# A streaming encoder layer on one core: two heads' prompt states computed behind the output projection, and the gated output turned one step later

## What is computed

```python
s_new = s * jnp.exp(L * log_gamma)[None, :, None, None] + jnp.einsum(
    'blhd,blhv->bhdv', k * k_decay[None, :, :, None], v)
```

## Time and profile before

| | us |
|---|---|
| median of 3 runs | 1492.9 |
| lowest and highest | 1490.93, 1495.36 |
| the profiled execution, its own time | 1492.03 |
| its span, first to last instruction | 1489.8 |
| TensorE busy | 1461.5 |
| VectorE busy | 837.7 |
| ScalarE busy | 659.5 |
| POOL busy | 303.2 |

### The profile page before, as it was taken

How to read it: one execution, slowest core, us unless ns; L and a number is a source line. 1 busy time by engine, 2 the same in 40 slices (tenths; PEclk the granted TensorE clock), 3 DMA queues, 4 the chain that set the end, 5 groups by cost and what they waited for, 6 DMA issues and landing times.

```text
span 1489.8 us, 21889 instructions
## 1 busy us (share of the span) xinstructions
PE 1461.5 (98%) x8004; PEld 1158.5 (78%) x8004; DVE 837.7 (56%) x1456; ACT 659.5 (44%) x1083; POOL 303.2 (20%) x181
## 2 busy tenths in 40 slices
PE   8999999999999999999999999999999999999998
PEld 6777787778777877787877677777888888887885
DVE  3532532253225222221866778655365899988998
ACT  5323312331233123322446545645233478888883
POOL 1352233224313431233000000000321100001004
PEclk9999999999999999999999999999999999999999
DMA  9646565555556455433441353245831799999996
GB/s 324 216 125 204 170 192 140 187 191 184 158 185 208 144 167 197 161 99 91 159 142 43 111 168 133 71 153 178 276 124 43 267 372 404 403 365 402 399 393 230
DMA packets 156460, 304.61 MB, mean 204 GB/s; under 512 B 16752, under 2 KB 54520, under 8 KB 155972
## 3 DMA queue, kind: packets, MB, share of 16 engines
q1 hardware_dynamic: 152548, 292.72, 58.2%
q0 software_dynamic: 3808, 10.49, 2.0%
HBM read 258.45 MB, written 47.86 MB: 206 GB/s over the span
## 4 chain that ended last, share of the span: by engine, by line
PE 45%; DMA 4%; DVE 2%; issue 1%; ACT 1%; POOL 0%; DVEq 0%; ACTq 0%; SPq 0%; POOLq 0%
PE pj L93 11%; PE pj L95 11%; PE pj L94 11%; DMA m_raw<-w 2%; PE d_B L2731 1%; PE d_B L2758 1%; PE d_B L2750 1%; DMA d_kc<-cache_diff_k 1%; PE d_B L2792 1%; PE d_B L2740 1%; PE d_B L2898 1%; PE d_B L2719 1%; PE d_B L1762 1%; PE d_B L2769 0%; PE pj L1745 0%
## 5 line engine op out<-in xcount | busy, mean ns | idle before, releaser
L93 PE MATMUL pj<-ring_hi,hT_hi 128*128 128x512 f32 x880 | 364.1, 414 | 3.7 <-ACT d_q_rows L2193 2.4
L95 PE MATMUL pj<-ring_hi,hT_lo 128*128 128x512 f32 x880 | 345.2, 392 | 0.0
L94 PE MATMUL pj<-ring_lo,hT_hi 128*128 128x512 f32 x880 | 344.0, 391 | 0.0
L546 POOL TENSOR_TENSOR ring_lo<-ring_raw,ring_hi 128x1024 fp32r<-128x1024 f32 x79 | 190.7, 2414 | 462.6 <-ACT ring_hi L628 462.5
L1622 DVE TENSOR_TENSOR m_lo<-m_raw,m_hi 128x1024 fp32r<-128x1024 f32 x188 | 222.1, 1221 | 18.8 <-ACT m_hi L1528 17.3
L628 ACT ACTIVATE ring_hi<-ring_raw 128x1024 fp32r<-128x1024 f32 x79 | 83.5, 1059 | 313.8 <-DMA ring_raw<-w_in 272.8
L1528 ACT ACTIVATE m_hi<-m_raw 128x1024 fp32r<-128x1024 f32 x188 | 192.0, 1058 | 19.9 <-DMA m_raw<-w 17.8
L93 PEld LDWEIGHTS pj<-ring_hi,hT_hi 128*128 128x128 f32 x880 | 166.2, 189 | 41.8 <-issue 8.9
L95 PEld LDWEIGHTS pj<-ring_hi,hT_lo 128*128 128x128 f32 x880 | 165.4, 188 | 36.1
L94 PEld LDWEIGHTS pj<-ring_lo,hT_hi 128*128 128x128 f32 x880 | 166.4, 189 | 29.3 <-issue 1.0
L853 DVE SCALAR_TENSOR_TENSOR r_S<-r_S,g,r_sm 128x512 f32<-128x512 f32 x64 | 45.0, 745 | 128.4 <-PE r_sm L1094 128.4
(11 more groups left out here) (403 smaller groups left out, 2507.4 us busy)
## 6 DMA issues: line engine op xcount, KB each, us to landing
m_raw<-w SPq DMA_DIRECT2D x188, 512.0 KB, 9.8
ring_raw<-w_in SPq DMA_DIRECT2D x72, 512.0 KB, 3.8
r_S<-state_ret SPq DMA_DIRECT2D x64, 256.0 KB, 4.7
r_ada_raw<-w_ada SPq DMA_DIRECT2D x16, 1024.0 KB, 6.6
o_state_s<-r_S SPq DMA_DIRECT2D x64, 256.0 KB, 3.3
a_raw<-w_ada SPq DMA_DIRECT2D x16, 512.0 KB, 8.7
ring_raw<-w_in SPq DMA_DIRECT2D x32, 256.0 KB, 3.4
ring_raw<-w_br_ret SPq DMA_DIRECT2D x16, 512.0 KB, 4.5
```

The costliest lines, as they stand in the source:

```text
L93: pe.matmul(out, s_hi, m_hi, start=start, stop=False)
L94: pe.matmul(out, s_hi, m_lo, start=False, stop=False)
L95: return pe.matmul(out, s_lo, m_hi, start=False, stop=stop)
L546: pool.tensor_tensor(lo[:, p], raw[:, p], hi[:, p].bitcast(F32), ALU.subtract).then_inc(lo_done, 1)
```

## The change

Heads 1 and 2 (`LATER`) no longer compute their prompt state in `phase_r`. Instead SP stores their operands (decayed keys high and low, values high and low, 3 MB a head) to memory, and ScalarE may take the next QK only when these stores have landed, as VectorE may turn it. In `phase_d`, when the output projection's operands have been used, SP loads them back in two halves a head, the products run between and behind the logits, where `stay_busy` had stood, ScalarE copies the results, and it issues their stores itself. For these two heads, `unit` and `cross` stand ahead of k = 2 in place of 1. For all heads, the turned tiles 0 and 1 come ahead of k = 6, 2 and 3 ahead of 7, and tile 4 at the start of BR; ScalarE copies that tile between QK's fourth and fifth bank.

```diff
+LATER = (1, 2)
...
+def later_home(io, i):
+
+    rows = io["yg"][4 * P + 6 * P * i:4 * P + 6 * P * (i + 1)]
+    return rows.rearrange("(p a) c -> p (a c)", p=P).rearrange("p (t c) -> p t c", t=NP_T)
...
+        def stored_for_later(eng, h):
+            if h - 1 in LATER:
+                eng.wait_ge(later_out, 64 * (LATER.index(h - 1) + 1))
...
+            def store_later(h):
+                sp.wait_ge(kd_low, h + 1)
+                for t in range(NP_T):
+                    bank_taken(sp, f"V{h}", t)
+                home = later_home(io, LATER.index(h))
+                sp.dma_start(home[:, :, 0:RDK], kd_hi[:].bitcast(F32)).then_inc(later_out, 16)
+                sp.dma_start(home[:, :, RDK:2 * RDK], qk_r[:, 0:NP_T, 1].bitcast(F32)).then_inc(later_out, 16)
+                sp.dma_start(home[:, :, W:2 * W], v_hi[:, 0:NP_T].bitcast(F32)).then_inc(later_out, 16)
+                sp.dma_start(home[:, :, 2 * W:3 * W], v_lo[:].bitcast(F32)).then_inc(later_out, 16)
...
                             if g + 1 < RH:
                                 load_tab(g + 1)
+                            if g in LATER:
+                                store_later(g)
...
-            def take(name, dst, func, done=None):
+            def take(name, dst, func, turned=None):
                 for t in range(NT):
+                    if t == NP_T and turned is not None:
+                        take_oT(turned, NP_T)
...
                     split_hi(b, 2)
-                    take_oT(h - 1, 4)
...
-                    take(first, lambda t: qk[:, t].rearrange("p a c -> p (a c)"), ACT.Copy)
+                    stored_for_later(act, h)
+                    take(first, lambda t: qk[:, t].rearrange("p a c -> p (a c)"), ACT.Copy, h - 1 if h else None)
...
             def in_qk(h, u, i):
-                if i == 1:
+                if i == (2 if h in LATER else 1):
                     unit(u)
                     cross(h, 2)
                     cross(h, 3)
-                elif 2 <= i <= 5:
+                if 2 <= i <= 5:
                     steps(h, 4 + 2 * i)
-                if i == 5:
-                    turn_o(h, 0)
...
+                if i >= 6:
+                    turn_o(h, 2 * i - 12)
+                    turn_o(h, 2 * i - 11)
+
+            def in_branch(h, u, i):
+                if i == 0:
+                    turn_o(h, NP_T)
+                elif i % 4 == 1:
                     unit(u + i // 4)
...
-                state(h, 0)
-                state(h, 1)
+                if h not in LATER:
+                    state(h, 0)
+                    state(h, 1)
...
+    def load_later(self, sp, i):
+        for a in range(2):
+            s = slice(2 * a, 2 * a + 2)
+            sp.dma_start(self.later[i][:, s].bitcast(F32), later_home(self.io, i)[:, s]).then_inc(self.later_in[i][a], 16)
+
+    def late_state(self, pe, i, t):
+        if t % 2 == 0:
+            pe.wait_ge(self.later_in[i][t // 2], 16)
...
+            last = mm3(pe, self.state_banks[i][d][:], w[:, t, s], w[:, t, low], w[:, t, W:2 * W], w[:, t, 2 * W:3 * W], t == 0, t == NP_T - 1)
...
+    def take_states(self, act, i):
...
+            act.dma_start(self.io["o_state_p"][0, 0, LATER[i], d * P:(d + 1) * P, :], self.states[i][d][:]).then_inc(self.state_out, 16)
...
             for t in range(NT):
+                if t == NT - 1:
+                    for i in range(len(LATER)):
+                        sp.wait_ge(w_done, 2 * NT - 1 + i)
+                        moe.load_later(sp, i)
                 sp.wait_ge(h2_done, 2 * t + 2)
...
-            stay_busy(8)
+            for b in (2, 3):
+                pe.wait_ge(pj_free[b], LAST + 2)
+            moe.late_state(pe, 0, 0)
             logits(3)
-            stay_busy(4)
+            moe.late_state(pe, 0, 1)
             for a in range(2):
                 turn_h2(4, a)
-            stay_busy(4)
             logits(4)
-            stay_busy(22)
+            for t in (2, 3):
+                moe.late_state(pe, 0, t)
...
+            for t in (0, 1):
+                moe.late_state(pe, 1, t)
             pe.wait_ge(assigned, 1)
...
+            for t in (2, 3):
+                moe.late_state(pe, 1, t)
             pe.wait_ge(moe.tok_done, 1)
-            stay_busy(5)
             moe.run_pe(pe)
```

More of the change, by code:

```diff
@@ L706, in _ @@
                             split_hi("V0", p)
[L707 removed]
+                    stored_for_later(act, h)
+                    take(first, lambda t: qk[:, t].rearrange("p a c -> p (a c)"), ACT.Copy, h - 1 if h else None)
                     split_hi(follow, 3)
                 else:
[L710 removed]
+                    stored_for_later(act, h)
+                    take(first, lambda t: qk[:, t].rearrange("p a c -> p (a c)"), ACT.Sigmoid, h - 1)
                     split_hi(f"BR{h - 1}", 3)
@@ L746, in _ @@
                 squares(h, 3)
-                for d in range(2):
-                    take_state(h, d)
+                if h not in LATER:
+                    for d in range(2):
+                        take_state(h, d)
             for p in range(3):
@@ L839, in take_T @@
                 if h and t == ROPE_ORDER[0]:
-                    dve.wait_ge(Sp_out, 32 * h)
+                    dve.wait_ge(Sp_out, 32 * len([g for g in range(h) if g not in LATER]))
+                    stored_for_later(dve, h)
                 dve.tensor_copy(qkT[:, :, t * P:(t + 1) * P], job_bank("T", h, t)[:].rearrange("p (k c) -> p k c", c=P)) \
@@ L1373, in __init__ @@
         self.U, self.V, self.Y, self.T, self.AT, self.X = banks[0], banks[1], banks[2:4], banks[4:6], banks[6], banks[7]
+        self.later = [nc.alloc_sbuf_tensor_at(f"m_later{i}", [P, NP_T, 3 * W], F32R, offset=(hT + 8192, wt)[i]) for i in range(len(LATER))]
+        self.states = [[nc.alloc_sbuf_tensor_at(f"m_state{i}_{d}", [P, W], F32, offset=base + 40960 + 2048 * (2 * i + d)) for d in range(2)]
+                       for i in range(len(LATER))]
+        self.state_banks = (banks[2:4], banks[0:2])
+        self.later_in = [many(f"later_in{i}_", 2) for i in range(len(LATER))]
+        self.state_done, self.state_taken, self.state_out = sem("state_done"), sem("state_taken"), sem("state_out")
         self.loaded0, self.hi0_done, self.lo0_done = many("first_loaded", 4), sem("first_hi_done"), sem("first_lo_done")
@@ L1448, in steps @@
             yield m, (m - 4) // 12, (m - 4) % 12
+    def load_later(self, sp, i):
[5 more added lines that the diff above has]
+            pe.wait_ge(self.later_in[i][t // 2], 16)
+        w = self.later[i]
+        for d in range(2):
+            s = slice(d * P, (d + 1) * P)
+            low = slice(RDK + d * P, RDK + (d + 1) * P)
+            last = mm3(pe, self.state_banks[i][d][:], w[:, t, s], w[:, t, low], w[:, t, W:2 * W], w[:, t, 2 * W:3 * W], t == 0, t == NP_T - 1)
+            if t == NP_T - 1:
+                last.then_inc(self.state_done, 1)
+    def take_states(self, act, i):
+        for d in range(2):
+            act.wait_ge(self.state_done, 2 * i + d + 1)
+            act.activation(self.states[i][d][:], self.state_banks[i][d][:], ACT.Copy).then_inc(self.state_taken, 1)
+        act.wait_ge(self.state_taken, 2 * i + 2)
+        for d in range(2):
+            act.dma_start(self.io["o_state_p"][0, 0, LATER[i], d * P:(d + 1) * P, :], self.states[i][d][:]).then_inc(self.state_out, 16)
     def load_first(self, sp):
@@ L1543, in take_y @@
                 act.wait_ge(*self.piece_used(r, first_piece("W2", e) + 2 * j + 1))
+                if e == 0 and j == 0:
+                    act.wait_ge(self.state_out, 64)
                 if e >= 2:
@@ L2886, in turn_h2 @@
                 last.then_inc(h_turned, 1)
-            def stay_busy(n):
-                for i in range(n):
-                    pe.matmul(pj[3][:, 0:P], K.ident[:], K.ident[:], start=True, stop=True)
             def logits(t):
```

28 lines of the change are left out of this document (16 added, 12 removed).

## The result

| | before | changed |
|---|---|---|
| median of five runs | 1492.9 us | 1500.67 us |
| lowest and highest | 1490.88, 1495.36 | 1499.84, 1502.34 |
| profiled execution: time, span | 1492.0, 1489.8 | 1499.84, 1497.7 |

The ratio is 1.0053 (95% interval 1.004 to 1.0066): slower by 7.8 us where 4.0 were forecast. It lies beyond the 0.3% that the prediction had called no change, on the slower side.

What follows compares the result with a forecast made beforehand. TensorE, busy 1461.5 of 1489.8 us, was taken as the bound. Terms -10.9 - 3.4 + 12.2 + 3.4 + 1.0 + 1.7 = +4.0 us on the median 1492.9 gave 1496.9 us, range 1487.5 to 1504.

Steps and rivals of the forecast that it cites:

- State products, -10.9: First phase: two heads' 24 matmuls each, 5.44 us a head, leave TensorE's path; -10.9 us.
- Turnings, -3.4: Turnings one step later: TensorE's waits of 0.7 and 0.16 us go at each of four borders; -3.4 us.
- The stall, +12.2: QK to BR border, two heads: TensorE waits 6.1 us each for ScalarE, behind queued stores and third weight piece; +12.2 us.
- the term for the piece behind the stores: SP's queue: BR's third weight piece, 0.52 MB at 328 GB/s, lands 1.6 us after the operand stores.
- Half clock behind the stall, +3.4: After each of the two border stalls TensorE runs at half clock, losing 1.7 us; +3.4 us.
- Cross products, +1.0: `unit` and `cross` of heads 1 and 2: the samples' states arrive 0.5 us late each; +1.0 us.
- Behind the output projection, +1.7: Way to the experts: last twelve products delay slot lists 0.8 us, stores beside the gather add 0.9; +1.7 us.
- 36 of the 48 products replace filler and cost nothing: Behind the output projection, ahead of the counts: 36 late state products take filler's place at no cost.
- From the first expert on, this delay stays.: Experts: TensorE is the bound again, so the +1.7 us from behind the output projection remains.
- the first (stores hidden): QK to BR border: stores and piece land before QK ends, no stall or slow clock; -11.6, 1481.3 us; chance 0.08.
- The third (slow stores): Operand stores: queue stays near 257 to 300 GB/s; with a stall of 9 us, +9.8, 1502.7 us; chance 0.25.
- my middle: QK to BR border: stall of 6.1 us, chosen between ends of 4.5 and 10 us set by store rates.

Runs made afterwards that it cites:

- Early stores: Changed kernel with SyncE issuing the four stores of a head's operands right behind the first branch piece, before the samples' states' stores and table; 1480.9 us, ratio 0.9918.
- turnings alone: Kernel before with only the gated output's turnings one step later, the fifth inside the branch products; state products stay in place; 1487.5 us, ratio 0.9961.
- the second run: Changed kernel with the operand stores issued right behind the first branch piece, run again unchanged; 1480.5 us, ratio 0.9927.

## Why the prediction was off by half, point by point

The sign and the place were right, and the time lies in the range. By the prediction's own bound the result is slower, to which it gave 0.40, and not unchanged, to which it gave 0.44. That the total is off by no more than 3.8 us is in part luck: the stalls with their clock cost 5.2 us more than forecast and the way to the experts 1.8 more, while the turnings gained 1.9 more and the experts took 2.8 less. Of the sum:

- **State products, -10.9.** Nearly right. Early stores less turnings alone is -9.0 and -7.9 in the state phase; without the waits that are left there (0.6 at the cross products and 0.4 at the branch products; 1.3 and 0.7 in the second run) it is -10.0 and -9.9. For the whole kernel the move is worth 1480.9 - 1487.5 = -6.6: it loses 4.2 on the way to the experts and finds 1.4 again in them.
- **Turnings, -3.4.** Too small: -5.3. The step took the waits as the list has them, and a listed wait leaves out the overlap that is lost with it.
- **The stall, +12.2.** The mechanism was right down to the engine, the piece and the queue; the size failed. Measured 8.1 and 8.5 us for a forecast of 6.1. In head 2 everything ran 2.1 us earlier than in the kernel before (the states' stores at 453.12, not 455.20), so the piece should have been seen by 469.0, and it was at 471.10. TensorE came when forecast (464.3; 466.6 - 2.1 = 464.5). What failed is mostly the term for the piece behind the stores. It was put at 1.6 us; ScalarE saw it 3.1 us behind the last store (2.5 in head 1). The stores themselves were only 0.6 late: seen at 468.0, where 468.7 + 0.85 - 2.1 = 467.5 was forecast. The rate taken for them held while they ran (409 GB/s from 462 to 464); the slow stretch, 241 GB/s, lies at 466 to 468, around the landing of the last store. Why the DMA is slow there is not shown. The forecast as a whole implied 358 GB/s (5.12 MB from 456 to 470.3), and 342 were measured over the 16 us.
- **Half clock behind the stall, +3.4.** Right: each distance of tile 4's turnings tells the whole price. From head 2 to head 3 it is 617.82 - 463.67 = 154.15 us against 143.48 with the turnings alone: 10.7, of which 8.7 are standing and 2.0 clock. Head 1's is 148.77 - 143.47, and the 5.44 of head 2's state products less the 0.6 of its cross products on top: 10.1. Together 20.8 for a forecast of 15.6.
- **Cross products, +1.0.** 0.7 and 0.6: 1.3.
- **Behind the output projection, +1.7.** 3.5. Both named parts came: the gather 1.0 later (8.7 against 7.7), the last twelve products 0.8 (counts to slots 4.07 against 3.31). The step that failed is "36 of the 48 products replace filler and cost nothing". The fillers also bridged the wait for ScalarE's copy ahead of the last logits; with the products there instead, in another order, 0.74 us stood open and the clock fell: 8.96 against 7.27 us to the counts, 1.7.
- **"From the first expert on, this delay stays."** It did not: the experts took 2.8 us less. In the eleven profiles they take 304.2 to 307.4, mostly less where the way to them was longer. Part of it can be read from TensorE's waits there, first in the kernel before, then in the changed one:

```profile
PE d_B L1762 <- DVE m_su L1657: 1.9, 2, 1.3
PE pj L93 <- DVE m_lo L1622: 0.8, 2, 0.5
```

```profile
PE d_B L1829 <- DVE m_su L1724: 0.9, 2, 0.5
```

From the first expert product on it waited 2.7 us for VectorE before and 0.9 with the change (m_lo, the weights' low parts, not at all): 1.8 of the 2.8. The profile with the longest experts, the turnings alone, has 3.1 us of such waits. That the waits are shorter because the weights and VectorE had more time is argued, not shown.
- **Not in the sum:** +1.2 us between the phase change and the logits. Of the eleven profiles this stretch has 445.8 to 448.7, those without late products no less than the others, and a wait of 1.1 us for `ring_lo` in the turnings-alone kernel too. I count it as the difference between executions, which is not shown.

The rivals: the first (stores hidden) describes exactly what the early stores do, and gave 1481.3; it measured 1480.9. The match is luck in part: the turnings gained 1.9 us more than in that sum, and the way to the experts cost 2.5 more. It was not the changed kernel's case because the argument against it held: 5 MB do not move in 8 us. The third (slow stores) was nearer than my middle in size: its stall of 9 us gives 1502.7, and the 8.3 found, with it, 1501.3. Its mechanism, a queue at 257 to 300 GB/s throughout, was not what ran.

## What to carry to other kernels

A product moved off the bound engine is paid for in bytes, so look in the profile for the stretch where the DMA is idle and the operands are already there, and issue the transfer in that stretch: the place of four stores in one queue was worth 20 us, twice what the move itself could win. In a queue with loads, cost a store by what lies behind it, and give the load behind the last store more than its bytes: it came 2.5 and 3.1 us later here, where its bytes at 328 GB/s gave 1.6. And before real work takes a filler's place, look which wait that filler bridged.

## What the runs showed of the hardware

- A wait of 0.74 us, with 16 narrow products behind it, was followed by half the clock (1.2 GHz) for some 3.5 us in three profiles (the changed kernel and the early stores twice), and the clock stayed at full in three others; a wait of 0.61 us was followed by half the clock too. I had thought of stalls of 2 us and more only.
- The half clock lasted for 14 products behind a stall of 4.4 us, and for ten behind one of 8.5 us.
- 38 small products of the identity kept the clock at full through 8 us of waiting, at DMA rates of 356 and 309 GB/s.
- Two stores of 256 KB beside a gather made it 8.1 to 8.8 us from its issue to the first use in seven profiles, against 7.7 to 7.8 in four without them.
